# Turning the gated product between the two down slots of an expert step

## The reference, cut to what matters

```python
def moe_swiglu(h, w_router, w_gate, w_up, w_down):
    ...
    for e in range(N_EXPERTS):                       # 8 experts
        y = (jax.nn.silu(t @ w_gate[e]) * (t @ w_up[e])) @ w_down[e]   # 1024 -> 3584 -> 1024
        out = out + combine[:, e:e + 1].astype(t.dtype) * y
```

## Time and profile before

| | us |
|---|---|
| median of 3 runs | 1363.68 (1361.87 to 1363.76) |
| the profiled execution | 1361.52 |
| its span in the trace | 1359.4 |
| granted TensorE clock over the span | 0.996 of full speed |
| TensorE busy | 1341.8 (99%) |
| VectorE busy | 1096.8 (81%) |
| ScalarE busy | 930.3 (68%) |
| GpSimd busy | 116.1 (9%) |

### The profile page before, as it was taken

How to read it: one execution, slowest core, us unless ns; L and a number is a source line. 1 busy time by engine, 2 the same in 40 slices (tenths; PEclk the granted TensorE clock), 3 DMA queues, 4 the chain that set the end, 5 groups by cost and what they waited for, 6 DMA issues and landing times.

```text
span 1359.4 us, 17436 instructions
## 1 busy us (share of the span) xinstructions
PE 1341.8 (99%) x7284; PEld 1133.0 (83%) x7285; DVE 1096.8 (81%) x748; ACT 930.3 (68%) x777; POOL 116.1 (9%) x138
## 2 busy tenths in 40 slices
PE   8999999999999999999999999999999999999997
PEld 8879999999678888888888888888888888888885
DVE  6766555567768888888888888888888988888996
ACT  6575333355767777777777777777777777777773
POOL 4310000002036400000000000000000000000010
PEclk9999999999989999999999999999999999999999
DMA  9746555545449999999999999999999999999993
GB/s 317 237 133 200 180 188 186 185 136 194 143 156 344 386 377 374 396 379 375 393 388 360 385 395 364 380 388 393 371 380 396 373 377 387 388 374 377 396 397 125
DMA packets 200548, 430.74 MB, mean 317 GB/s; under 512 B 9688, under 2 KB 46192, under 8 KB 200464
## 3 DMA queue, kind: packets, MB, share of 16 engines
q1 hardware_dynamic: 195088, 415.37, 84.3%
q0 software_dynamic: 4512, 13.45, 2.7%
q10 hardware_dynamic: 864, 0.74, 0.2%
HBM read 417.54 MB, written 7.35 MB: 313 GB/s over the span
## 4 chain that ended last, share of the span: by engine, by line
PE 97%; DVE 1%; ACT 1%; DMA 0%; issue 0%; ACTq 0%; DVEq 0%
PE ps L1349 94%; PE ps L1640 2%; PE ps L1622 0%; PE ps L1375 0%; PE ps L1507 0%; ACT hT_both L704 0%; DMA work_b<-in_ffn_norm_g 0%; ACT work_a L826 0%; DVE hT_both L990 0%; DVE xr L1245 0%; DVE w_low L977 0%; ACT work_a L742 0%; ACT w_high L696 0%; PE ps L1473 0%; DVE w_low L1030 0%
## 5 line engine op out<-in xcount | busy, mean ns | idle before, releaser
L977 DVE TENSOR_TENSOR w_low<-raw,w_high 128x2048 fp32r<-128x2048 f32 x387 | 892.0, 2306 | 171.0 <-ACT w_high L696 170.5
L696 ACT ACTIVATE w_high<-raw 128x2048 fp32r<-128x2048 f32 x390 | 747.1, 1916 | 290.2 <-PE ps L1349 290.2
L1349 PE MATMUL ps<-w_high,hT_both 128*128 128x512 f32 (+1 forms) x1920 | 600.1, 390 | 0.0
L1349 PEld LDWEIGHTS ps<-w_high,hT_both 128*128 128x128 f32 x1920 | 359.8, 189 | 71.5
L1349 PE MATMUL ps<-w_low,hT_both 128*128 128x512 f32 (+1 forms) x960 | 370.9, 386 | 0.0
L1349 PE MATMUL ps<-w_high,act_both 128*128 128x512 f32 x1072 | 343.4, 391 | 1.8 <-DVE act_both L1237 1.8
L1349 PEld LDWEIGHTS ps<-w_high,act_both 128*128 128x128 f32 x1072 | 202.1, 189 | 43.7 <-DVE act_both L1237 2.1
L1349 PEld LDWEIGHTS ps<-w_low,hT_both 128*128 128x128 f32 x960 | 181.2, 189 | 34.7
L1349 PE MATMUL ps<-w_low,act_both 128*128 128x512 f32 x536 | 209.4, 391 | 0.0
L1349 PE MATMUL ps<-hT_both,w_high 128*128 128x256 f32 x960 | 177.6, 284 | 2.0 <-DVE hT_both L990 1.0
L1349 PEld LDWEIGHTS ps<-hT_both,w_high 128*128 128x128 f32 x960 | 151.3, 192 | 4.0 <-issue 2.5
(11 more groups left out here) (269 smaller groups left out, 665.1 us busy)
## 6 DMA issues: line engine op xcount, KB each, us to landing
raw<-in_moe_w_gate SPq DMA_DIRECT2D x112, 1024.0 KB, 7.8
raw<-in_moe_w_up SPq DMA_DIRECT2D x112, 1024.0 KB, 7.7
raw<-in_moe_w_down SPq DMA_DIRECT2D x112, 1024.0 KB, 7.7
raw<-in_w_in SPq DMA_DIRECT2D x13, 1024.0 KB, 5.7
raw<-in_dense_w_gate SPq DMA_DIRECT2D x11, 1024.0 KB, 5.5
raw<-in_dense_w_up SPq DMA_DIRECT2D x11, 1024.0 KB, 5.4
raw<-in_dense_w_down SPq DMA_DIRECT2D x11, 1024.0 KB, 4.9
raw<-in_w_out SPq DMA_DIRECT2D x8, 1024.0 KB, 7.4
```

Of the source, the lines that this page charges most:

```text
L696: act.activation(w_part[0][:, s % PART_RING, :], raw[:, s % RAW_RING, :], ACT.Copy).then_inc(w_high_done, 1)
L977: dve.tensor_tensor(w_part[1][:, q, :], raw[:, r, :], w_part[0][:, q, :], ALU.subtract).then_inc(w_low_done, 1)
L1349: return pe.matmul(out_, lhsT, rhs, start=start, stop=stop, skip_group_check=True)
```

## The change

In every step but the last, TensorE's wait on `prod_done` and the four transposes of `turn_act` move from behind the second down slot to between the two. For ScalarE and VectorE nothing moves in steps 0 to 54. The activations of step 55 move: the copy on ScalarE and the subtraction on VectorE, which stood behind `high(t+7)` and `low(t+7)` of step 54, now stand between `high(t+6)` and `high(t+7)`, and between `low(t+6)` and `low(t+7)`. The branch for experts with more than 128 tokens (`i` not None) gets the first edit and not the second.

```diff
@@ ScalarE
+            def act_copy(n, k, i, per_n):
+
+                act.wait_ge(act_turned, at(i, per_n, n + k + 1))
+                act.activation(act_part[0][:, k % 2, :], ps[:, 2, :], ACT.Copy).then_inc(act_high_done, 1)
+
...
                     if not last:
                         high(t + 2, i, per_s)
-                    act.wait_ge(act_turned, at(i, per_n, n + k + 1))
-                    act.activation(act_part[0][:, k % 2, :], ps[:, 2, :], ACT.Copy).then_inc(act_high_done, 1)
+                    if not last or i is not None:
+                        act_copy(n, k, i, per_n)
...
                         high(t + 6, i, per_s)
+                        if i is None and k == experts * EG - 2:
+                            act_copy(n, k + 1, i, per_n)
                         high(t + 7, i, per_s)
@@ VectorE
+            def act_low(n, k, i, per_n):
+
+                dve.wait_ge(act_high_done, at(i, per_n, DG + n + k + 1))
+                dve.tensor_tensor(act_part[1][:, k % 2, :], ps[:, 2, :], act_part[0][:, k % 2, :], ALU.subtract).then_inc(act_low_done, 1)
+
...
                     if not last:
                         low(t + 2, i, per_s)
-                    dve.wait_ge(act_high_done, at(i, per_n, DG + n + k + 1))
-                    dve.tensor_tensor(act_part[1][:, k % 2, :], ps[:, 2, :], act_part[0][:, k % 2, :], ALU.subtract).then_inc(act_low_done, 1)
+                    if not last or i is not None:
+                        act_low(n, k, i, per_n)
...
                     low(t + 6, i, per_s)
+                    if i is None and k == experts * EG - 2:
+                        act_low(n, k + 1, i, per_n)
                     low(t + 7, i, per_s)
@@ TensorE
                     for j in range(2):
                         w = slot(t + (0 if last_step else 4) + j, 2, i, per_s)
+                        if j == 1 and not last_step:
+                            pe.wait_ge(prod_done, at(i, per_n, DG + n + k + 2))
+                            turn_act()
                         for f in range(2):
                             for hf in range(2):
                                 last = terms(...)
                         last.then_inc(w_used, 1)
-                    if not last_step:
-                        pe.wait_ge(prod_done, at(i, per_n, DG + n + k + 2))
-                        turn_act()
```

## The result

Over 13 runs of each on one chip the changed kernel takes 1365.03 us (median; 1362.81 to 1367.87), the kernel before 1362.33 us (1360.19 to 1363.76). The medians are 2.7 us apart; the ratio of the runs is 1.0025, 95% interval 1.0017 to 1.0033. The interval lies wholly above 1, so the kernel got slower, by little. The forecast was 1365.1 us. That the figures meet is partly luck: it was counted from the 1363.68 us of three runs, and the growth that was forecast is 1.4 us, half of the one measured. The profiled execution has a span of 1364.3 us, 4.9 more than before.

A forecast was written before the change was run, and what follows sets the result against it. TensorE was taken to bound the kernel; 0 + 0.4 (gather steps) + 0.7 (expert ends) + 0.3 (end) = +1.4 us on the 1363.68 us median gave 1365.1 us, range 1362.2 to 1367.6.

The forecast's parts named there:

- What bounds the kernel: Whole kernel: TensorE sets the time, weights arrive early enough; the expert stage has no idle time to take away.
- three signs of being wrong: Ordinary steps of 16.9 us or more, a `high` waiting for a transfer, or the slow clock inside the expert stage.
- The turns cost nothing: All 55 moved turns: the four transposes take the same 0.44 us wherever they stand; forecast 0.
- Ordinary steps, 0: Wait on `prod_done` in 48 steps without a gather: room 0.34 us exceeds 0.11 us handover and restart; cost nothing.
- the rival with waits in 48 steps: `prod_done` holds TensorE in ordinary steps too, losing weight-load head start: 1369.9 us, or 1375.7 if all lost; chance 0.12.
- Gather steps, 0.4 us: Wait on `prod_done` in seven gather steps: TensorE waits 0.06 us each, 0.4 us together; upper bound 1.9 us.
- Room 0.05 us, cost 0.11 us: Gather steps: product ends 0.05 us before the turns would start, handover and restart take 0.11, so TensorE waits 0.06 us.
- Behind expert ends, 0.7 us: Steps behind seven expert ends: later copy to `y_sb` delays `high` and `low`; 0.1 us each, 0.7 together, bound 2.1 us.
- 535.61, just in time: Behind expert ends: `low(t+2)` with handover at 535.61 meets the 25th `gate_up` matmul at 535.62; only the 37th is late, 0.07 us.
- The end, 0.27 us: End of step 54: the 0.61 us subtraction leaves the last path, 0.87 us of turns and copy enter; +0.27 us.
- Clock: Slow stretch behind the last wait: no change forecast; rivals 1.6 us longer (chance 0.06) or 1.6 us shorter (0.05).
- The forecast of no measurable change: Whole kernel: 0.1% more, within the 0.2% (2.7 us) that measurement can tell; chance 0.82.

The follow-up runs named there:

- both causes hidden: Changed kernel, ScalarE's copy to `y_sb` behind the next `high(t+2)`, gather-step product ahead of the two subtractions; 1.0007 of before.
- deferred wait alone: Kernel before, step 55's down slots taken in turn, `low(t+7)` awaited behind 12 matmuls; no ratio, stage 896.31 us, end 18.87 us.
- deferred wait: Kernel with turns moved in step 54 alone and second edit; step 55 awaits `low(t+7)` behind 12 matmuls; 0.9992, again 0.9982 of before.

## Why the prediction was right, and where it was too small

*What bounds the kernel.* Right: no idle time was there to be had in the stage, and none of the experiments took its 896.31 us lower. None of the three signs of being wrong came: ordinary steps of the kernel after are 16.79 to 16.82 us (step 0 reads 16.90, 0.09 of it by where its first matmul is counted from), every idle microsecond of ScalarE ahead of its `high`s (293.2 us) ended with TensorE, and the granted clock is 1.00 from the first turns to the last wait.

*The turns cost nothing.* Right: with both causes hidden the stage is 0.4 us over before, less than 0.01 us for each move.

*Ordinary steps, 0.* Right: with 0.34 us of room no wait appears, of turns or of their weight loads, and the rival with waits in 48 steps has fallen. Its head start argument (the load is due 0.22 us ahead) left it 0.06 us of margin, and that was enough.

*Gather steps, 0.4 us.* The place was right and the size too small: 0.97 us by undoing it. The room was as forecast (product 0.05 us ahead of the turns); the step that failed is "Room 0.05 us, cost 0.11 us". The 0.11 is from a wait in which TensorE had run dry, and there it holds (0.12 to 0.13 in the run with turns after 9 matmuls). For a near tie it is 0.19.

*Behind expert ends, 0.7 us.* Again the place right, the size half: 1.38 us. The step that failed is "535.61, just in time": it asked whether `low` was there before the matmul, where it has to be there before the matmul's weight load. So both waits cost, the one at the 25th and the one at the 37th matmul, and not the second alone. The head start of a load is 0.22 us, so up to 0.22 us could be lost at each of the 14 late loads; it was 0.10 us for each (1.38 / 14). The Trainium skill ("TensorE: Matmul & The Clock Gate", section "Architectural detail: the array is 16× 32×32, not 1× 128×128") says that TensorE's queue can pull weight loads ahead of running matmuls. The trace agrees, in that the loads run 0.22 us ahead where nothing holds them.

*The end, 0.27 us.* Right: 0.33 to 0.35, and the chain as described. That the second edit alone does it was not separated in the prediction; undoing it shows it.

*Clock.* "No change" holds for the profiled execution. As a rival it was put wrongly, as a matter of the idle time's length: the slow stretch comes and stays away with 1.8 us of idle time and with 2.2 (last section). That a longer gap speaks for a longer slow stretch was the prediction's own step, and no run shows it.

*The sum.* 0.97 + 1.38 + 0.34 = 2.7 us by experiment, 0.2 untraced, 2.9 in the trace, 2.7 between the medians. The forecast of no measurable change had 0.82 for it. The ratio lies just past the line that I drew for it (0.2%, 1.0020), its interval on both sides, and with 13 runs of each a smaller change than that line could be told: the kernel is slower. The measured median is 0.1 us under the forecast because two errors met: the median of three runs that it was counted from was 1.35 us above that of 13, and the growth was 1.3 us too small. One bound of the range was also added up wrongly. The upper bounds of gather steps and expert ends together give 1365.1 + 1.5 + 1.4 = 1368.0 us, above the 1367.6 that was to hold them.

## What to carry to other kernels

Where a matmul waits for another engine, compare the end of what it waits for with the start of its weight load, not with its own. A tie within a tenth of a microsecond cost 0.10 us each time here behind expert ends and 0.14 in gather steps, and a step that is moved past one slot meets such ties in the rare steps (a gather, a copy out), not in the common one. When something is taken off the last path, see whether the engine at its end can start with a part of the work: the second edit, together with the turns of step 54, was worth something (1.3 and 1.5 us between the medians) only with a wait that was split in two. A median of three runs can be off by a microsecond (1363.68 us of three, 1362.33 of thirteen); differences of that size are read from one and the same stretch of two traces.

## What the hardware showed that I had not expected

The slow clock behind the last wait is not there in every execution. With 2.2 us of idle time, the traces of the kernel after, with the turns back at expert ends and with the move in step 54 alone have it; those with the turns back in gather steps and with both causes hidden have not. With 1.8 us, the traces of before, without the second edit and with the deferred wait alone have it, and that with the turns after 9 matmuls has not (17 matmuls in 4.0 us at full clock). So six traces have it and three have not, and the length of the idle time does not divide them. The stretches of the kernel with the turns back in gather steps, 18 matmuls in 4.0 us at full clock (2.4 GHz) behind the same wait:

```profile
1344.40:1346.70 2.30, 0.14 (x2) 0.04 (x1) 2.15 (x1) 0.00 (x0) 0.00 (x0) 1.00 0.00 0
1346.70:1350.70 4.00, 4.00 (x18) 3.29 (x19) 0.33 (x1) 0.60 (x1) 0.00 (x0) 1.00 0.00 0
```

From step 54's first `gate_up` to the last addition this is 29.60 us instead of 31.16. The kernel with both causes hidden also had none (29.56). So the 1.6 us are paid in some executions, and a kernel that takes the idle time away gains them only in those. For the deferred wait this leaves less than the 3.3 us that its first trace gained up to the last addition: about 1.7 us where before has no slow stretch either (30.96 - 1.6 = 29.4, against 27.64). The medians gained 1.3 and 1.5, a little less still. The intervals reach to 2.3 and 3.7 us and so allow it, but that the clock is the whole reason isn't shown. A part of what a trace gains there can also be lost behind the last addition: in the first trace of the deferred wait the last store took 4.0 us from issue to landing, in that of before 3.2, and of the 3.3 us 2.5 were left at the end of the span.
